# Norms of a two-layer decoder trunk: the squares of two channel blocks are added on VectorE or GpSimd before one ones matmul takes both

## What is computed

```
def rmsnorm(x, g):
    y = xf * lax.rsqrt(jnp.mean(xf * xf, axis=-1, keepdims=True) + EPS)
    return y * g
for l in range(DEPTH):                       # 2
    h = rmsnorm(x, norm_mix_g[l])            # mixer: pooling, attention, gating
    ...
    x = x + merged @ w_out[l]
    hx = rmsnorm(x, norm_xattn_g[l])         # cross-attention to 256 memory tokens
    ...
    x = x + o @ w_xo[l]
    hf = rmsnorm(x, norm_ffn_g[l])           # squared-ReLU MLP, 1024 -> 4096 -> 1024
    x = x + jnp.square(jax.nn.relu(hf @ w_ff1[l])) @ w_ff2[l]
return rmsnorm(x, final_norm_g)
```

## Time and profile before

| what | value |
|---|---|
| median of 3 runs | 2398.74 us (2395.89 to 2828.28) |
| the profiled execution | 2399.41 us |
| its span, slowest core (core 6) | 2397.7 us |
| spans of the 8 cores | 2388.7 to 2397.7 us |
| TensorE busy | 2294.2 us, 96% |
| VectorE, ScalarE, GpSimd busy | 1153.8, 957.7, 211.3 us |

### The profile page before, as it was taken

One profiled execution on the slowest core, in us unless ns is written; L12 is line 12 of the kernel. 1 busy time (PEld: TensorE's weight loads), 2 busy tenths in 40 slices (PEclk: granted clock), 3 DMA queues, 4 the chain that ended last, 5 costly groups with the idle time before them and its releaser, 6 DMA issues.

```text
span 2397.7 us, 37862 instructions; the slowest of 8 cores (2388.7 to 2397.7 us)
## 1 busy us (share of the span) xinstructions
PE 2294.2 (96%) x13806; PEld 1149.6 (48%) x14032; DVE 1153.8 (48%) x1825; ACT 957.7 (40%) x1472; POOL 211.3 (9%) x240
## 2 busy tenths in 40 slices
PE   5899999999999999999999999999999999999997
PEld 1466554444444444444456655444444444444444
DVE  3456654443545534344474664444444454434346
ACT  4677763223533211112267767232353440302124
POOL 4200110000101000000020001000000000000001
PEclk8899999999999999999999999999999999999998
DMA  7421683335500333332552049332342022322304
GB/s 172 63 29 20 89 133 36 36 36 82 76 10 1 40 40 36 41 39 36 129 92 29 11 76 112 70 45 36 58 76 35 1 27 36 45 36 36 44 1 141
DMA packets 170292, 128.86 MB, mean 54 GB/s; under 512 B 6912, under 2 KB 143488, under 8 KB 170112
## 3 DMA queue, kind: packets, MB, share of 16 engines
q0 software_dynamic: 139680, 80.92, 28.1%
q1 hardware_dynamic: 30432, 45.51, 7.3%
HBM read 190.14 MB, written 16.78 MB: 86 GB/s over the span
## 4 chain that ended last, share of the span: by engine, by line
PE 91%; ACT 3%; DVE 3%; issue 3%; DMA 0%; SPq 0%; ACTq 0%; POOL 0%; DVEq 0%; POOLq 0%
PE ps L485 91%; ACT pb L436 1%; DVE A L449 1%; ACT sq L436 0%; DVE x L449 0%; DMA x<-xT 0%; ACT ps L436 0%; DVE hm L449 0%; ACT rstd L436 0%; DVE kT L461 0%; ACT aT L436 0%; DVE vz L461 0%; ACT P L436 0%; DVE E L723 0%; DVE E L442 0%
## 5 line engine op out<-in xcount | busy, mean ns | idle before, releaser
L485 PE MATMUL ps<-A,wsl 128*128 128x512 bf16 x3749 | 846.4, 380 | 12.5 <-DVE A L449 3.8
L485 PEld LDWEIGHTS ps<-A,wsl 128*128 128x128 bf16 x3840 | 374.0, 98 | 458.1 <-issue 18.1
L485 PE MATMUL ps<-hid,wsl 128*128 128x512 bf16 (+2 forms) x2137 | 447.1, 368 | 7.5 <-DVE x L442 5.5
L436 ACT ACTIVATE T<-ps 128x512 f32<-128x512 f32 x288 | 171.2, 596 | 630.3 <-PE ps L485 615.4
L442 DVE TENSOR_TENSOR x<-ps,x 128x512 f32<-128x512 f32 (+2 forms) x336 | 221.3, 665 | 316.2 <-PE ps L485 300.4
L485 PEld LDWEIGHTS ps<-hid,wsl 128*128 128x128 bf16 x2176 | 210.2, 99 | 242.2 <-issue 6.0
L436 ACT ACTIVATE pb<-ps 128x1024 bf16<-128x1024 f32 (+1 forms) x320 | 275.8, 895 | 61.4 <-PE ps L485 59.7
L442 DVE TENSOR_TENSOR hid<-T 128x512 bf16<-128x512 f32 x256 | 176.2, 692 | 251.3 <-ACT T L436 251.3
L449 DVE SCALAR_TENSOR_TENSOR T<-T,ps 128x512 f32<-128x512 f32 x160 | 107.1, 686 | 246.3 <-PE ps L485 211.7
L436 ACT ACTIVATE sq<-x 128x512 bf16<-128x512 f32 (+2 forms) x240 | 132.1, 594 | 170.0 <-PE ps L485 128.3
L436 ACT ACTIVATE T<-ps,halfb 128x512 f32<-128x512 f32 x128 | 87.9, 687 | 244.0 <-PE ps L485 241.1
(11 more groups left out here) (131 smaller groups left out, 1988.1 us busy)
## 6 DMA issues: line engine op xcount, KB each, us to landing
wsl<-w_ff POOLq DMA_DIRECT2D x64, 512.0 KB, 7.0
x<-xT SPq DMA_DIRECT2D x64, 256.0 KB
wsl<-w_in POOLq DMA_DIRECT2D x30, 512.0 KB, 10.4
wsl<-w_xkv POOLq DMA_DIRECT2D x16, 512.0 KB, 10.5
xsave<-x SPq DMA_DIRECT2D x32, 256.0 KB
x<-xsave SPq DMA_DIRECT2D x32, 256.0 KB
wsq<-w_qkv POOLq DMA_DIRECT2D x24, 256.0 KB, 6.6
outT<-x SPq DMA_DIRECT2D x24, 256.0 KB
```

What stands on the lines that cost most here:

```text
L436: P.add("act", [lambda h: h.activation(out=o, in_=i_, func=func, scale=sc, bias=bi)], [out], [in_] + more, 175 + 0.833 * size(out) + 90 * ...
L485: fns.append(lambda h, o=o, l_=l_, r_=r_, start=start, stop=stop, kw=kw: h.matmul(o, lhsT=l_, rhs=r_, start=start, stop=stop, **kw))
```

## The change

Two squares go as float32 into two T tiles, VectorE or GpSimd adds them into the `sq` tile, and one ones matmul takes the sum. The tuple PAIR names the engine of the four adds of a norm. It is used in `norm_x` (cross-attention norm of tiles 0 and 1, MLP norm of tile 3, mixer norm of the second layer), in the MLP norms of tiles 0 to 2, and in the final norm of tiles 0 to 2. The mixer norms of the first layer, the cross-attention norms of tiles 2 and 3, the memory norm and the final norm's three pieces stay as they were. The px buffers change too: the T tiles are used for token tile 0 alone, and eight buffers in 16 KB at MR + 16384 for the rest.

```diff
-        def norm_tile(src, gcol, dst, bank=None, tw=TT, aside=()):
+        def norm_tile(src, gcol, dst, bank=None, tw=TT, aside=(), pair=()):
             b = banks() if bank is None else bank
-            for dc in range(8):
+            step = 2 if pair else 1
+            for dc in range(0, 8, step):
                 s_ = Sq()
-                act(s_[:, 0:tw], src(dc), AF.Square)
-                mms([(ps[:, b, 0:tw], ones_bf[:, :], s_[:, 0:tw], dc == 0, dc == 7, {})])
+                if pair:
+                    two = (T(), T())
+                    for i in range(2):
+                        act(two[i][:, 0:tw], src(dc + i), AF.Square)
+                    tt(s_[:, 0:tw], two[0][:, 0:tw], two[1][:, 0:tw], ALU.add, eng=pair[dc // 2])
+                else:
+                    act(s_[:, 0:tw], src(dc), AF.Square)
+                mms([(ps[:, b, 0:tw], ones_bf[:, :], s_[:, 0:tw], dc == 0, dc + step == 8, {})])
...
+        PAIR = ("pool", "dve", "pool", "dve")
+
         def norm_x(t, gcol):
-            norm_tile(lambda dc: xsl(dc, t), gcol, lambda dc: Asl(dc, t))
+            norm_tile(lambda dc: xsl(dc, t), gcol, lambda dc: Asl(dc, t), pair=PAIR)
...
-            xm = Area(MR + 24576, 8192)
-            px_rr = RR([place("px", [128, 2, 512], BF16, t_.base) for t_ in Tg] + [xm.put("px", [128, 2, 512], BF16) for i in range(4)])
+            xm = Area(MR + 16384, 16384)
+            px_t = [place("px", [128, 2, 512], BF16, t_.base) for t_ in Tg]
+            px_m = RR([xm.put("px", [128, 2, 512], BF16) for i in range(8)])
...
-                p_ = px_rr()
+                p_ = px_t[hh] if t == 0 else px_m()
...
-                    norm_tile(lambda dc: xsl(dc, t - 2), vb + 52, lambda dc: Asl(dc, t - 2), bank=xo_b())
+                    norm_tile(lambda dc: xsl(dc, t - 2), vb + 52, lambda dc: Asl(dc, t - 2), bank=xo_b(), pair=PAIR)
...
-                    norm_tile(part, VPL * DEPTH, part, tw=w, aside=(1, 4, 6) if t >= 2 else ())
+                    norm_tile(part, VPL * DEPTH, part, tw=w, aside=(1, 4, 6) if t >= 2 else (), pair=PAIR if t < 3 else ())
```

## The result

The changed kernel takes 2404.55 us (median of 6, 2403.67 to 2613.19), the kernel before 2397.3 in the same session: ratio 1.0033, 95% interval 1.0019 to 1.0048. It is slower by 0.3%, well inside the 2% that count as no change, but outside my range (2375 to 2393) and on the other side of no change. The profiled execution took 2405.9 us.

A forecast was written before the change was run, and what follows sets the result against it. TensorE, busy 96% of the span, was taken as the bound. -16.4 (matmuls) + 0.3 (MLP starts) + 0.7 (end) + 0.5 (elsewhere) = -14.9 from 2399.4, forecasting 2384.5 us at chance 0.64, range 2375 to 2393.

The forecast's parts named there:

- the first term: In 19 paired norms, 76 ones matmuls go at 0.216 us each: 16.4 us less of TensorE.
- Rival 4: Removed ones matmuls stood in TensorE's waits, so no matmul time is saved; chance 0.16 together with rival 2.
- the +0.3 of the MLP starts: TensorE idle 4.0 us instead of 3.3 at the first start, 4.3 instead of 4.7 at the second; bounds -8, +5.
- the +0.5 for all places outside the three named: VectorE slowed by GpSimd's adds outside the two MLP starts and the end: +0.5 us, bounds 0 and +42.
- My 2.6 us for GpSimd's first add at the first start: First MLP start: TensorE waits 2.6 us for tile 3's first add behind a memset, then some 1.3 us again.
- VectorE's loss of 1.1 us per meeting: VectorE loses 1.1 us for each GpSimd operation beside it; 42 us if all 38 adds met it.
- the bound of the MLP starts: Upper bound +5 us, if both adds of a start wait for VectorE's block of eight products (5.38 us).
- rival 2: Some 11 GpSimd adds collide with VectorE's products at MLP starts and end: 12 us, to 2396.5; chance 0.16 with Rival 4.
- rival 3: GpSimd's add uncovered in every norm: 47.5 us lost, 2430.5; wins from 0.86 us per norm; chance 0.05.
- Rival 1: Cores 4 and 6 lose their extra wait near 1480:1500, 7 us off, to 2377.5; chance 0.12.
- The end: Final norms: VectorE's chain gains 1.0 us instead of the 1.7 of saved matmuls, so +0.7; bounds -1, +3.5.
- px: Buffers after the output projection: T tiles freed from tile 2 on, new buffers free as early as the old; nothing.

The follow-up runs named there:

- b4: Changed kernel with each x reload waiting for one mg block, every second square left out of the sum and no adds: ratio 0.9908 to the kernel before.
- b3: Changed kernel with the x reloads spread over the merge, each waiting for one block of mg: ratio 0.9976 to the kernel before.
- d1: c3 with each pair taking two places of the T-tile ring and using one, so the ring holds two pairs: ratio 0.9923 to the kernel before.
- c3: b3 with the two squares of a pair written as bf16 into the halves of one T tile: ratio 0.9923 to the kernel before.
- a1: Kernel before with only the px buffers changed, no pairing and no adds: ratio 1.0024 to the kernel before.
- a2: Changed kernel with 61 one-column matmuls at its very start, shifting TensorE's later instructions: ratio 1.0072 to the kernel before.
- c4: c3 with all adds on VectorE (bf16 squares, spread x reloads): ratio 0.9900 to the kernel before.
- b6: b3 with all 76 adds on VectorE (float32 squares, spread x reloads): ratio 0.9989 to the kernel before.

## Why the prediction was wrong

**Bound and removal: right.** TensorE is the bound, and b4 shows the 76 matmuls worth at least the 16.4 us of the first term. Rival 4 falls.

**Two terms of the sum failed, and each weighs about 10 us.** One is the +0.3 of the MLP starts: their stretches came out +0.5 and -0.6 us where -4.5 and -5.6 were forecast, 10.0 together. The other is the +0.5 for all places outside the three named, which I took from near the lower end of its bounds (0 and +42): the mixer norms came out +6.8 us instead of -3.5. The sign of being wrong that the prediction itself names, a wait for GpSimd ahead of a ones matmul in the second layer's mixer norms, is there on all eight cores (4.17 us on core 0).

**The MLP starts: "The 152 squares stay; I count no change", and an add is "hidden".** The squares' durations did not change (627 ns against 622), their time did. Going through float32 T tiles, two to an add, a square can only be made when an older pair has been added, and each add stands in the queue of an engine that is late just at the MLP starts. I priced an add as 0.69 us and a semaphore behind the last square; beside GpSimd's, VectorE's adds took 871 ns on the mean. Measured against b4, where the first square of a pair also goes straight to TensorE, the adds with their T tiles cost 6.4 and 9.6 us at the two starts. The size of the operands carries 3.5 and 4.6 us of it (b3 to d1; 10.4 over the kernel), the ring nothing at the first start and 3.4 at the second (d1 to c3; 3.2 over the kernel).

**The MLP starts, wait by wait.** My 2.6 us for GpSimd's first add at the first start measured 1.68, the 1.3 behind it did not come there; at the second I had 4.3 us, and 2.25 were for GpSimd, 1.51 for VectorE's add. What I left out are the waits ahead of them: 2.15 and 1.55 us for px, 2.00 and 2.59 us for A, and two half-clock stretches of 3.4 us at the first start on core 0. My window had 3.3 us idle in before (core 6, and core 0 the same); core 0 of after has 60 - 53.15 = 6.9 us, and TensorE's clock fell with it:

```profile
core 0: us, PE busy (x) PEld busy (x) DVE busy (x) ACT busy (x) POOL busy (x), PEclk, DMA share, GB/s
740.00:800.00 60.00, 53.15 (x228) 22.72 (x227) 40.50 (x57) 21.83 (x39) 13.05 (x9) 0.94 0.14 17
```

The px wait of the first start is in b4 too (2.19 us on core 0) and not in a1: it comes with the matmuls that are gone ahead of it, and neither with the adds nor with the px buffers alone.

**VectorE and GpSimd together: the mechanism right, one direction left out.** VectorE's loss of 1.1 us per meeting was confirmed (1.68 us for an add of 0.69 in the mixer norms; 6.40 instead of 5.38 for a block in b3). I bounded only VectorE's side. GpSimd shut out through a whole block, 5.1 us, was in the bound of the MLP starts, and I kept it from the mixer norms, where it happened: +6.8 instead of -3.5 with the clock's fall behind it. The rule of the Trainium skill that I cited ("SBUF — State Buffer", section "Who interferes with whom") was a warning of more than I made of it; the same section has it that issue order decides who is blocked, and the 0.3 us between after and b3 agree in kind. It speaks of one instruction, which here would be 0.67 us of waiting; the long add was held up through the block, 5.1 us, and the measurement decides. It was my rival 2 and a piece of rival 3 at one norm of 19, not all: the point from which rival 3 decides, 0.86 us per norm, was passed on the average through three places.

**Rival 1 the wrong way round.** I saw the gap of core 6 at 1486 us, did not ask what it was, and wrote that the change doesn't touch that place. It does: 76 matmuls less (40 of them ahead of it) move what stands at instruction 20,922 some 60 matmuls on, into the x reloads. The mean cost of the stop is 5.1 to 5.5 us (255.7 against 250.6 in a2 or 250.2 in b3), on the slowest core up to 9.5 (259.0 against 249.5). Against before only 1.9 of it is seen, since that kernel has 251.8 us on its undisturbed cores and this one 249.5; why, no run shows.

**The end:** -1.2 against -1.9, right in kind and near in size. **px:** nothing, confirmed.

Together: the forecast lost 5.0 us at each MLP start, 10.3 in the mixer norms and 1.9 in the stretch of the code's stop, 0.7 at the end: 22.9, less 0.6 gained ahead of the first mg and 0.5 that I had set aside. That is the 21.8 us between my -14.9 and the measured +6.9 of mean span.

Open is what part of the half-clock stretches each wait carries by itself, what shifts ScalarE by the 0.3 us in b3, and what holds up the code's packet among the x reloads. Moving the one long add to VectorE in the mixer norm was not tried, since it would stand there behind the same eight products.

## What to carry over

Removing work from the bound engine pays its price only if what replaces it is early at the places where that engine waits: ask of each new operation how long it takes beside its neighbours, what stands ahead of it in its engine's queue, and then which buffer its producer waits for. Two-byte intermediates made VectorE's adds short enough that the trade paid in every stretch with paired norms (c4; 2.4 GHz matmuls of 0.216 us against 0.42 us of VectorE with time to spare). Where an engine stops with no releaser, count instructions and look for the packets of kind "instruction": if the stop stays at the same number of the stream, or a multiple of 256 from it, and ends just behind such a packet, it is the code that comes late. Both moving the code and spreading the DMAs that it meets helped here; either can bring up a stop at another block.

## What the runs showed that I had not expected

- A GpSimd add of two float32 tiles took 1.28 us alone, 1.53 us beside eight VectorE products if it started 1.00 us behind them and 6.38 us if it started 0.72 us behind, in 16 of 16 and 24 of 24 cores; at 0.4 to 0.6 and at 1.7 us behind it was short too.
- TensorE stops of up to 6.8 us at fixed numbers of its instruction stream, 98 of them in eighteen profiles and all a multiple of 256 apart, each of the 70 longest ending 1.1 to 1.6 us behind a packet of 16,384 bytes of code; at number 20,922 on seven cores of eight in after, on none with the code moved by 61 matmuls.
- Behind the waits of 4 to 7 us the granted clock was 0.50, 1.2 GHz, for 3.4 or 6.8 us (longer at the end of the program): eight matmuls took 3.57 us instead of 1.89. Half of such a stretch is lost on top of the wait.
- VectorE adds two bf16 tiles of 512 columns in 0.42 us on the mean and two float32 tiles in 0.69 where GpSimd adds none (c4 and b6), 0.72 and 0.87 where it does (c3 and after); GpSimd gained much less, 1.15 against 1.33 us (c3 and b3).
